# Value tiles of two weight chunks as one wide product, and weight units dealt out by one table, in a two-layer encoder kernel

## The reference, cut to what matters

```
for i in range(2):
    x = x + 0.5 * swiglu(rmsnorm(x), w_ffn1_gu[i], w_ffn1_down[i])
    h = rmsnorm(x)
    x = x + (even_mixer if i == 0 else odd_mixer)(h @ w_in, ...) @ w_out
    x = x + 0.5 * swiglu(rmsnorm(x), w_ffn2_gu[i], w_ffn2_down[i])
    x = x + sigmoid(rmsnorm(x) @ w_ple_gate[i]) * (p[i] @ w_ple_proj[i])
```

## Time and profile before

| | us |
|---|---|
| median of 3 runs | 1041.66 (1041.18 to 1042.16) |
| the profiled execution | 1041.61 |
| its span in the trace | 1039.9 |
| PE busy in it | 1028.7 |
| DVE, ACT, POOL busy | 757.4, 588.3, 51.7 |

### The profile page before, as it was taken

One profiled execution on the slowest core, in us unless ns is written; L12 is line 12 of the kernel. 1 busy time (PEld: TensorE's weight loads), 2 busy tenths in 40 slices (PEclk: granted clock), 3 DMA queues, 4 the chain that ended last, 5 costly groups with the idle time before them and its releaser, 6 DMA issues.

```text
span 1039.9 us, 18263 instructions
## 1 busy us (share of the span) xinstructions
PE 1028.7 (99%) x6596; PEld 922.2 (89%) x6596; DVE 757.4 (73%) x1350; ACT 588.3 (57%) x1001; POOL 51.7 (5%) x100
## 2 busy tenths in 40 slices
PE   9999999999999999999999999999999999999997
PEld 8888888999888888888998888889997888888897
DVE  5988765768658887765888787657666787786566
ACT  6666545546646665554666565445664665654463
POOL 1000001000011000000110000000000200000000
PEclk9999999999999999999999999999999999999999
DMA  9675457784316655457647554578633375645741
GB/s 319 219 233 163 142 159 211 218 268 134 125 52 201 204 179 180 131 167 230 215 141 238 194 185 139 144 206 276 207 92 121 124 238 195 198 128 151 204 165 41
DMA packets 225383, 185.52 MB, mean 178 GB/s; under 512 B 3664, under 2 KB 223536, under 8 KB 225200
## 3 DMA queue, kind: packets, MB, share of 16 engines
q1 hardware_dynamic: 222832, 180.94, 55.5%
q10 hardware_dynamic: 2496, 3.86, 1.0%
HBM read 183.59 MB, written 1.07 MB: 178 GB/s over the span
## 4 chain that ended last, share of the span: by engine, by line
PE 97%; DVE 1%; issue 1%; ACT 1%; DVEq 0%; POOL 0%; ACTq 0%; POOLq 0%
PE ps L1430 42%; PE ps L1435 22%; PE ps L1341 5%; PE ps L1342 4%; PE ps L1343 4%; PE ps L1350 4%; PE ps L1545 2%; PE ps L1546 2%; PE ps L1547 2%; PE ps L1351 2%; PE ps L1621 1%; PE ps L1634 1%; PE ps L1662 1%; PE ps L1640 1%; PE ps L1789 1%
## 5 line engine op out<-in xcount | busy, mean ns | idle before, releaser
L898 DVE TENSOR_TENSOR wsp<-raw,wsp 128x1024 fp32r<-128x1024 f32 (+1 forms) x381 | 416.4, 1109 | 61.4 <-ACT wsp L591 60.7
L591 ACT ACTIVATE wsp<-raw 128x1024 fp32r<-128x1024 f32 (+1 forms) x381 | 354.5, 958 | 24.1 <-PE ps L1343 19.9
L1430 PE MATMUL ps<-xsA,wsp 128*128 128x512 f32 x976 | 232.8, 391 | 0.0
L1430 PEld LDWEIGHTS ps<-xsA,wsp 128*128 128x128 f32 x976 | 179.3, 188 | 34.9
L1430 PE MATMUL ps<-hff,wsp 128*128 128x512 f32 x616 | 145.0, 390 | 0.0
L1430 PEld LDWEIGHTS ps<-hff,wsp 128*128 128x128 f32 x616 | 113.8, 188 | 22.8
L1435 PEld LDWEIGHTS ps<-xsA,wsp 128*128 128x128 f32 x976 | 125.0, 191 | 4.6
L1435 PE MATMUL ps<-xsA,wsp 128*128 128x256 f32 x976 | 126.8, 283 | 0.0
L913 DVE TENSOR_TENSOR sq<-ps,sq 128x512 f32<-128x512 f32 x88 | 60.5, 687 | 87.5 <-ACT sq L607 87.1
L607 ACT ACTIVATE sq<-ps 128x512 f32<-128x512 f32 x88 | 51.9, 590 | 110.8 <-PE ps L1435 109.2
L653 ACT ACTIVATE xsA<-xT,gains 128x256 fp32r<-128x256 f32 x48 | 24.4, 508 | 135.2 <-DVE xT L1047 120.4
(11 more groups left out here) (217 smaller groups left out, 1425.5 us busy)
## 6 DMA issues: line engine op xcount, KB each, us to landing
raw<-in_w_ffn_gu_dram SPq DMA_DIRECT2D x87, 1024.0 KB, 5.1
raw<-in_w_ffn_down_dram SPq DMA_DIRECT2D x64, 704.0 KB, 4.7
raw<-in_w_in_even_dram SPq DMA_DIRECT2D x11, 1024.0 KB, 5.5
raw<-in_w_in_odd_dram SPq DMA_DIRECT2D x9, 1024.0 KB, 5.3
raw<-in_w_ple_gate_dram SPq DMA_DIRECT2D x8, 1024.0 KB, 5.9
raw<-in_w_out_even_dram SPq DMA_DIRECT2D x4, 1024.0 KB, 5.1
raw<-in_w_out_odd_dram SPq DMA_DIRECT2D x4, 1024.0 KB, 5.7
raw<-in_w_ple_proj_dram SPq DMA_DIRECT2D x2, 1024.0 KB, 5.0
```

The costliest lines, as they stand in the source:

```text
L591: act.activation(wsp[:, s, 0, half * n:(half + 1) * n], raw[:, s, half * n:(half + 1) * n], ACT.Copy).then_inc(hi, 1)
L898: dve.tensor_tensor(wsp[:, s, 1, sl], raw[:, s, sl], wsp[:, s, 0, sl].bitcast(F32), ALU.subtract).then_inc(lo, 1)
L1430: pe.matmul(ps[:, bank, :], whi, moving.rearrange("p s t -> p (s t)"), start=first and i == 0, stop=False)
```

## The change

Where a group's two value chunks are next to each other in the order (layer 0 group 1, layer 1 group 0), their four tiles become two products, one for each token block, with 512 moving columns that are taken from two ring slots at once. Each product is written as two tiles of the list, `half` (blocks k 0 to 3) and `vv` (k 4 to 7), which add up in one PSUM bank, so that the number of tiles and the place of the attention steps stay. ScalarE copies 512 columns after `vv` and nothing after `half`. Both chunks must be ready at the first of the four tiles, and both are released after the fourth.

`paced_units` makes one table of units by attention step: at most one unit more per step, and never beyond what the slots allow. ScalarE and VectorE both follow it, in `mixer_in` and in the first half of `mixer_out`.

The core of the diff:

```diff
+def chunks_of(tile):
+    chunk, _, what, idx, _ = tile
+    return (idx[2], idx[2] + 1) if what in ("half", "vv") else (chunk,)
...
         for what, j in order:
+            if what == "v" and layer != group:
+                if j == 0:
+                    for t in range(TOK):
+                        tiles.append((chunk, 0, "half", (group, t, chunk), 1.0))
+                        tiles.append((chunk + t, 0, "vv", (group, t, chunk), 1.0))
+                chunk += 1
+                continue
...
-            ends += [T + sum(t[0] <= r for t in tiles) for r in range(ph.chunks)]
+            ends += [T + max(n + 1 for n, t in enumerate(tiles) if r in chunks_of(t)) for r in range(ph.chunks)]
...
-            ends = n + 1 == len(tiles) or tiles[n + 1][0] > tiles[n][0]
+            ends = all(tiles[n][0] not in chunks_of(t) for t in tiles[n + 1:])
...
+        def paced_units(layer):
+            c0 = [ph.c0 for ph in phases if (ph.kind, ph.layer) == ("in", layer)][0]
+            out0 = [ph.c0 for ph in phases if (ph.kind, ph.layer) == ("out", layer)][0]
+            ph_in = [ph for ph in phases if (ph.kind, ph.layer) == ("in", layer)][0]
+            first, n_in = FIRST_SLOT[layer], len(IN_TILES[layer])
+            done, table = in_units(ph_in, first - 1), []
+            for i in range(SLOTS):
+                target = in_units(ph_in, first + i) if first + i < n_in else 2 * (out0 + RING)
+                done = max(done, min(target, done + 1))
+                table.append(done)
+            return [in_units(ph_in, first - 1)] + table
...
-        def in_bank(n):
+        def in_bank(layer, n):
+            if IN_TILES[layer][n][2] == "vv":
+                n -= 1
             return n % 4 if n < 8 else (n - 8) % 3
...
# ScalarE, mixer_in
-                        if what == "v":
+                        if what == "vv":
+                            group, t, _ = idx
+                            start, w = GROUP_W * group, 2 * 256
+                        elif what == "v":
...
                     for i in slots(ph.layer, n):
                         attention_step(ph.layer, i)
-                        advance(in_units(ph, n))
+                        advance(paced_units(ph.layer)[i + 1])
...
# ScalarE, mixer_out
-                    advance(2 * (ph.c0 + RING))
+                    advance(paced_units(ph.layer)[i + 1] if out_slots(ph.layer, m) else 2 * (ph.c0 + RING))
...
# VectorE, mixer_in
-                        attention_step(ph.layer, i, in_units(ph, n - 1))
+                        attention_step(ph.layer, i, paced_units(ph.layer)[i])
...
# VectorE, mixer_out
-                        attention_step(ph.layer, i, 2 * (ph.c0 + RING) - (m == 0))
+                        attention_step(ph.layer, i, paced_units(ph.layer)[i])
                     next_tile()
                     dve.tensor_tensor(xT[:, m], ps[:, out_bank(ph.layer, m), 0:SEQ], xT[:, m], ALU.add).then_inc(half_resid, 1)
-                    advance(2 * (ph.c0 + RING))
+                    advance(paced_units(ph.layer)[i + 1] if out_slots(ph.layer, m) else 2 * (ph.c0 + RING))
...
# TensorE
-            def token_tile(out_, t, xs, weights):
-                for k in range(KD):
+            def token_tile(out_, t, xs, weights, ks=range(KD)):
+                for k in ks:
...
-                    chunk_ready(c)
-                    reuse(bank)
-                    if what in "qk":
+                    chunk_ready(ph.c0 + chunks_of(IN_TILES[ph.layer][n])[-1])
+                    if what != "vv":
+                        reuse(bank)
+                    if what in ("half", "vv"):
+                        s, ks = (ph.c0 + idx[2]) % RING, range(KD // 2) if what == "half" else range(KD // 2, KD)
+                        pair = wsp[:, s:s + 2] if s < RING - 1 else wsp[:, ::-(RING - 1)]
+                        mm = token_tile(ps[:, bank, :].rearrange("p (c n) -> p c n", c=2), idx[1], xs,
+                                        lambda k: pair[:, :, :, k * 256:(k + 1) * 256].rearrange("p c s n -> p s c n"), ks)
+                        mm.then_inc(tile_done, 1)
+                    elif is_qk(what):
...
-                    pe.wait_ge(*last_written(layer, lambda what, idx: what == "v" and idx[:2] == (group, h // 4)))
+                    pe.wait_ge(*last_written(layer, lambda what, idx: (what == "v" and idx[:2] == (group, h // 4)) or (what == "vv" and idx[0] == group)))
```

More of the change, by code:

```diff
@@ L401, in is_v, with is_qk @@
             return what[0] == "v"
+        def is_qk(what):
+            return what in "qk"
         def written(layer, n):
@@ L407, in written @@
             v = is_v(tiles[-1][2])
-            return (v_ready if v else qk_ready), sum(is_v(t[2]) == v for t in tiles)
+            return (v_ready if v else qk_ready), sum((is_v if v else is_qk)(t[2]) for t in tiles)
         def last_written(layer, want):
@@ L716, in mixer_in @@
                         act.wait_ge(rcol_ready, norm + 1)
-                        act.activation(vN[:, t, start:start + w], ps[:, in_bank(n), 0:w], ACT.Copy,
+                        act.activation(vN[:, t, start:start + w], ps[:, in_bank(ph.layer, n), 0:w], ACT.Copy,
                                        scale=rcol[:, t:t + 1]).then_inc(v_ready, 1)
@@ L1058, in forget_gate @@
                     dve.wait_ge(*written(0, n))
-                    dve.scalar_tensor_tensor(fl[:, t], ps[:, in_bank(n), 256:W_FORGET], rcol[:, t:t + 1], bf[:], ALU.mult, ALU.add).then_inc(f_biased, 1)
+                    dve.scalar_tensor_tensor(fl[:, t], ps[:, in_bank(0, n), 256:W_FORGET], rcol[:, t:t + 1], bf[:], ALU.mult, ALU.add).then_inc(f_biased, 1)
                 dve.wait_ge(f_biased, TOK)
@@ L1068, in mixer_in @@
                         inverse_root(norm, ahead=2)
-                    bank = in_bank(n)
+                    bank = in_bank(ph.layer, n)
                     next_tile()
-                    if not is_v(what):
+                    if is_qk(what):
                         dst = (qT if what == "q" else kT)[:, idx, :]
@@ L1562, in mixer_in @@
                 for n, (chunk, col, what, idx, scale) in enumerate(IN_TILES[ph.layer]):
-                    bank, c = in_bank(n), ph.c0 + chunk
-                    chunk_ready(c)
-                    reuse(bank)
-                    if what in "qk":
+                    bank, c = in_bank(ph.layer, n), ph.c0 + chunk
+                    chunk_ready(ph.c0 + chunks_of(IN_TILES[ph.layer][n])[-1])
[8 more added lines that the diff above has]
+                    elif is_qk(what):
                         tile8(bank, c % RING, col, xs, KD * norm if n == 0 else None, xs_lo)
@@ L1574, in mixer_in @@
                         token_tile(ps[:, bank, 0:w], t, xs, lambda k: view[:, :, k, col:col + w]).then_inc(tile_done, 1)
-                    reader[bank] = (f_biased, idx[2] + 1) if with_forget(ph, chunk) else written(ph.layer, n)
+                    if what != "half":
+                        reader[bank] = (f_biased, idx[2] + 1) if with_forget(ph, chunk) else written(ph.layer, n)
                     if n == 0:
```

## The result

The changed kernel takes 1044.11 us (median of 12 runs, 1043.93 to 1045.81) against 1041.37 us for the kernel before in the same jobs (1041.13 to 1042.16). The ratio is 1.0028, with a 95% interval of 1.0021 to 1.0035: it is slower by 0.28%. The forecast was 1042.3, within 1040.4 to 1043.6, and no change most likely. The profiled execution took 1044.16 us, its span is 1042.4 us, 2.5 us longer than before's.

A forecast was written before the change was run, and what follows sets the result against it. PE was taken to bound the kernel, busy 1028.7 of 1039.9 us. The terms -1.07 (wide products) + 0.93 + 0.84 (stalls) = +0.70 us gave 1042.3 us, range 1040.4 to 1043.6.

The forecast's parts named there:

- The wide products: Per mixer, 96 value-tile matmuls of 256 columns become 48 of 512 at 228 ns: 1.07 us less in both.
- The stalls: Output projection, unit after half tile 2 (layer 0) and 1 (layer 1): new PE waits, +0.84 and +0.93 us.
- The value copies: ScalarE, value tiles: four copies of 256 columns become two of 512, 0.66 us less per mixer, hidden: 0.
- The copy of tile 23: Layer 0, before step 12's values product: copy of 0.59 us fits by 0.1 us; taken as 0, else some 0.4.
- Nothing outside the mixers: Rest of the kernel, including the start: the sum has only mixer terms, and nothing downstream absorbs it.
- Both chunks early, both released late: Second chunk ready two tiles sooner, slots released two tiles later, in both layers: units still come in time, 0.
- the bank: PSUM bank 2, both layers: needed again 3 us after the product, against a copy of 0.6 us: 0.
- the later loads: SP's last two loads of each mixer come one or two half tiles later, read over 20 us later: 0.
- Rival 1: Output projection: the new waits don't show, VectorE having slack or ScalarE's unit coming sooner; 1040.6 us, chance 0.2.
- Rival 2: Value tiles: the wide pace, about 0.24 us a matmul, gains nothing; 1043.4 us, chance 0.1.
- rival 3: Wide matmuls: the jump between two slots costs; decisive at 14 ns, 1045.2 us at 30 ns; chance 0.08.
- rival 4: Wide matmuls overlap: needs 29 ns off 228 each; 1031.9 us if one costs as a 256-column one; chance 0.02.

The follow-up runs named there:

- experiment 5: Changed kernel with early table load, a unit table that catches up, and VectorE's last two units of layer 1 held back: 1040.37 us, ratio 0.9987.
- experiment 3: Kernel before, narrow value tiles, with ScalarE's and VectorE's units at the changed kernel's late steps: 1042.97 us, ratio 1.0015.
- experiment 2: Changed kernel with ScalarE's table of exponentials loaded early, after tile 7 of layer 1: 1043.16 us, ratio 1.0020.
- Experiment 7: Kernel before, 96 or 48 matmuls left out: 1036.91, 1039.06 us; changed kernel with early load and catch-up table, plus 200 memsets or 96 small matmuls: 1048.47, 1055.81 us.
- experiments 1 and 4: 1: changed kernel run again, 1044.46 us. 4: changed kernel with early table load and a unit table that catches up, 1041.62 us, ratio 1.0005.

## Why the prediction was wrong

**The wide products: right in kind, too large.** Forecast 1.07 us for both mixers; measured 0.30 to 0.32 us in layer 0 and 0.46 us in layer 1 (tiles 8 to 11 last 13.99 us in experiment 5 against 14.45), 0.77 us together. The pace was 230 ns and not 228, which is small for a matmul and large for the saving: what a wide one saves is 2 x 119.5 - 230 = 9 ns instead of 11, 0.43 us per mixer instead of 0.53. Layer 1 has that (0.46). In layer 0 the four tiles are 0.40 us shorter (3.04 to 2.94 us each), and 0.1 us is lost again in the steps between them. By the Trainium skill's section that the forecast names ("Back-to-back issue gap"), the isolated gap would have put the saving at 0.12 us per mixer, the sustained one at 5.2 us; the measurement is near neither.

**The stalls: right.** Forecast 0.84 us in layer 0 and 0.93 in layer 1; measured +0.74 and +0.77, at the steps named, and experiment 3 has both, 1.48 us in all, without the rest of the change. I had given each 0.1 to 0.2 us for a restart that the timeline does not show. In layer 1 that was a misreading: the 0.48 us behind a block of transposes that had waited ran to a values product, the 0.30 us of the other block to a half tile. The changed kernel's block at 796.52, which waited 0.69 us and has a half tile behind it, takes 0.31 us.

**The value copies: the step that failed.** I wrote that the copies are 0.66 us less on ScalarE, "hidden, since ScalarE isn't what PE waits for there", and took 0. The time of the copies is indeed hidden. But the copy that vanished after tile 8 had carried a wait, and with it gone the table load moved behind the logits: 1.03 us on PE (the +0.57 of the account and the 0.46 that the tiles there are shorter), shown by experiment 2 (15.02 to 13.99 us). The copy of tile 23, which I had found tight, took 0.69 us and not 0.59, began at 280.14 and fitted by 0.06 us.

**Nothing outside the mixers: also wrong.** The sum had no term for the first 16 us, since no instruction there changes. Measured: 0.91 us in the pair of profiles. Experiment 7 ties the slow transfers behind it to the number of matmuls in PE's program, which the forecast itself gave as 6500, as a detail to look for. The size is less firm than the kind: over the eleven profiles without the late ones the averages differ by 0.67 us.

**What was safe, was.** Both chunks early, both released late, the bank, the later loads: no wait of PE's is at any of these places. With every term at its measured size the sum is -0.77 + 0.74 + 0.77 + 1.03 + 0.91 = +2.68 us, against 2.74 between the medians and 2.55 between the two profiled executions from which the terms are read. So 0.1 us of the sum is in no term.

**The rivals.** Rival 1 (no stalls) fell with experiment 3. Rival 2 (no gain from the wide pace), rival 3 (a jump between slots, which needed 14 ns a matmul) and rival 4 fell with the 230 ns, 2 above the pace of one slot. The 0.03 for something else was what happened.

## What to carry to other kernels

When an edit removes an instruction, ask what else was tied to it: a wait that it carried, and any instruction that the compiler places by it, such as a table load. Load a table explicitly, as soon as the last use of the old one is past; here that gave back 1.03 us on PE. Weight work in a queue is best placed behind what the bound engine wants next; here two units of VectorE, held back by two half tiles, were worth more than the wide products. And compare the first microseconds of the two profiles too, even where the source there is the same.

## What was not expected of the hardware

The rate of the first transfers goes with the length of PE's instruction stream: with 6500 matmuls 221 to 251 GB/s between 4 and 6 us, with 6548 or more 365 to 401 GB/s, in 14 of 14 profiles, with wide or narrow tiles.

A second effect comes with it. Of 61 timed executions of the kernels with 6500 matmuls 22 have a span that is 1.3 us or more over the shortest of the same kernel. Of 55 executions of the experiments with more matmuls 3 do, all of the kernel with 96 small ones, and of 94 executions of the kernel before one does. Three profiles with 6500 matmuls are of such executions: those of experiments 1 and 4, and the one with 96 matmuls left out. In the first, the eight transposes after the wait for xin take 1.97 us, against 1.10 us in the changed kernel's:

```profile
7.39 1.97 PE L1845 MATMUL ps<-ident,xin 128*128 128x128 f32 x8 [0.64 <-DMA xin<-in_x_dram]
```

The column of the granted clock says 1.00 in both, but it has nothing to go by there. The trace's records of the clock begin, at full level, only at 6.05 us of the changed kernel's profile and at 11.09 us of this one, and ahead of its first record the column reads 1.00. In the three late profiles the records begin at 10.73 to 11.16 us and the first matmul of 512 columns starts at 11.19 to 11.45 us; in the other eleven it is 4.44 to 6.94 us and 8.69 to 9.97 us. So the late executions that were profiled are those in which PE gets its full clock late. PE has waits there in late and in other profiles alike, so why it does in some executions only, and why so much more often with 6500 matmuls, is open. A granted clock of 1.00 in the first microseconds of a profile is no proof of full speed: look at how long the matmuls take.
